# Scan of a two-layer backbone on one core: the order of two products, and level evictions of only the changed columns

## The reference

```python
def wkv_scan(state, r, w, k, v, a, b, reverse):
    def step(s, inp):
        r_t, w_t, k_t, v_t, a_t, b_t = inp
        sa = jnp.einsum('bhij,bhj->bhi', s, a_t)
        s = s * w_t[:, :, None, :] + sa[..., None] * b_t[:, :, None, :] + v_t[..., None] * k_t[:, :, None, :]
        return s, jnp.einsum('bhij,bhj->bhi', s, r_t)
    tm = lambda t: jnp.swapaxes(t, 0, 1).astype(jnp.float32)
    state, y = lax.scan(step, state, tuple(tm(t) for t in (r, w, k, v, a, b)), reverse=reverse)
    return state, jnp.swapaxes(y, 0, 1)
```

## Time and profile before

| | us |
|---|---|
| median of 3 runs | 2361.94 (2360.23 to 2364.19) |
| the profiled execution | 2363.53 |
| its span, first to last instruction | 2361.7 |
| first and last r of the scan begin (line 2023) | 1284.6 and 2213.7 |
| period, m4 to m4, latent | 11.80 |
| mean granted TensorE clock | 0.972 of full |

### The profile page before, as it was taken

How to read it: one execution, slowest core, us unless ns; L and a number is a source line. 1 busy time by engine, 2 the same in 40 slices (tenths; PEclk the granted TensorE clock), 3 DMA queues, 4 the chain that set the end, 5 groups by cost and what they waited for, 6 DMA issues and landing times. The chain is left out here.

```text
span 2361.7 us, 56008 instructions
## 1 busy us (share of the span) xinstructions
PE 2152.6 (91%) x23820; PEld 1377.2 (58%) x23820; DVE 1160.8 (49%) x2245; ACT 803.0 (34%) x2060; POOL 623.4 (26%) x882
## 2 busy tenths in 40 slices
PE   7999999999699989999895898999999898989798
PEld 3556555355344444544344777777777777777543
DVE  4122122134647670042523666666666666666574
ACT  4111111133245522210112444444444544444332
POOL 0000000023022410011113444444444444444111
PEclk9999999999799999999996999999999999999899
DMA  8200002600027755455313343333333333333542
GB/s 350 112 27 27 18 27 80 232 27 27 30 65 209 196 139 180 146 176 187 133 60 112 83 151 88 88 89 94 85 96 85 92 86 89 87 89 79 188 142 107
DMA packets 313562, 258.50 MB, mean 109 GB/s; under 512 B 138593, under 2 KB 271969, under 8 KB 309858
## 3 DMA queue, kind: packets, MB, share of 16 engines
q1 hardware_dynamic: 313314, 254.92, 35.8%
HBM read 175.13 MB, written 79.69 MB: 108 GB/s over the span
## 5 line engine op out<-in xcount | busy, mean ns | idle before, releaser
L876 PE MATMUL ps<-xt,w_slab 128*128 128x512 f32 (+1 forms) x832 | 312.0, 529 | 10.2 <-DVE xt L1156 10.2
L432 PE MATMUL ps<-h,fw_slab 128*128 128x512 f32 (+1 forms) x768 | 282.0, 527 | 2.1 <-ACT h L259 2.1
L1973 PE MATMUL ps<-M,AT 64*64 64x64 f32 x6400 | 272.0, 225 | 5.0 <-DVE M L1860 2.1
L1719 POOL TENSOR_TENSOR SP<-Q,decay 64x128 f32<-64x128 f32 x304 | 139.2, 458 | 467.2 <-DVE Q L1900 438.0
L876 PEld LDWEIGHTS ps<-xt,w_slab 128*128 128x128 f32 x832 | 155.6, 191 | 162.9 <-issue 136.4
L1973 PEld LDWEIGHTS ps<-M,AT 64*64 64x64 f32 x6400 | 221.3, 136 | 48.5 <-issue 14.9
L1973 PE MATMUL ps<-TT,MT 64*64 64x64 f32 x5120 | 218.0, 225 | 20.4 <-ACT XT L1781 15.3
L432 PEld LDWEIGHTS ps<-h,fw_slab 128*128 128x128 f32 x768 | 145.7, 191 | 133.0 <-issue 125.4
L1973 PEld LDWEIGHTS ps<-TT,MT 64*64 64x64 f32 x5120 | 179.2, 136 | 51.3 <-issue 38.2
L1846 DVE COPY_PREDICATED TT<-mask,ps 128x256 f32<-128x256 int32 x400 | 167.2, 435 | 77.3 <-PE ps L1973 74.7
L1889 DVE STREAM_TRANSPOSE MT<-M 128x256 f32<-128x256 f32 x240 | 106.9, 445 | 148.9 <-ACT M L1781 146.4
(11 more groups left out here) (266 smaller groups left out, 3187.0 us busy)
## 6 DMA issues: line engine op xcount, KB each, us to landing
feat<-feature_scratch SPq DMA_DIRECT2D x160, 256.0 KB, 3.2
feature_scratch<-k_feats SPq DMA_DIRECT2D x64, 320.0 KB, 5.1
feature_scratch<-k_feats SPq DMA_DIRECT2D x24, 640.0 KB, 6.7
k_feats<-in_modw SPq DMA_DIRECT2D x8, 1536.0 KB, 6.4
w_slab<-in_rwin SPq DMA_DIRECT2D x24, 512.0 KB, 6.8
Q<-v_token_scratch SPq DMA_DIRECT2D x320, 32.0 KB, 2.5
Z<-v_token_scratch SPq DMA_DIRECT2D x320, 32.0 KB, 2.2
fgo<-in_modw SPq DMA_DIRECT2D x8, 1024.0 KB, 7.8
```

The costliest lines, as they stand in the source:

```text
L432: mm = pe.matmul(ps[:, b0 + b, 0:n], wi[:, half, k, :], h0[:, k, a:a + n], start=k == 0, stop=k == KT - 1)
L876: mm = pe.matmul(ps[:, bank, 0:n], w[:, i % 2, k, :], src[:, k, a:a + n], start=k == 0, stop=k == KT - 1)
L1719: g.tensor_tensor(SP[own(h)], turn(sub, Q[l][own(h), h]), pend_turn(c, own(h), sub).unsqueeze(2).broadcast_to([HD, NDIR, CK]), ALU.mult).t ...
L1973: mm = pe.matmul(out[o, b, :], L[o, b, :], R[o, b, :], start=True, stop=True)
```

## The change

1. On PE, `state(j, c, 0)` goes in front of `y_state(j, c, 0)`. The wait for Z goes with it. The second half of the period (sub 1) keeps its order.
2. M and TT tiles are evicted only in the columns that the level changes: in each 2k columns the first k in the forward direction and the second k in reverse, 128 of 256 columns, in runs of k (k = 2, 4, 8, 16, 32). M and TT tiles get k or CK columns of padding so that one access pattern covers both directions. The eviction of mt32 writes 128 columns (runs of 32) into MT, and XT is gone; `sa` reads MT. The mask table shrinks to 256 + 5 x 128 = 896 columns. The masking of MT1, its transpose and the transposes to MT keep their 256 columns.

```diff
+NMASK = 256 + 128 * len(LEVELS)
...
-    maskf = sb("mask_in", [P, 6, 256])
-    mask = sb("mask", [P, 6, 256], I32)
+    maskf = sb("mask_in", [P, NMASK])
+    mask = sb("mask", [P, NMASK], I32)
...
-    AT, MT1, M, MT, XT = ([sb(f"{n}{s}", [P, B4, CK]) for s in two] for n in ("AT", "MT1_", "M", "MT", "XT"))
-    TT = {k: [sb(f"TT{k}_{s}", [P, B4, CK]) for s in two] for k in LEVELS}
+    AT, MT1, MT = ([sb(f"{n}{s}", [P, B4, CK]) for s in two] for n in ("AT", "MT1_", "MT"))
+    M_cols = [sb(f"M{s}", [P, B4 * CK + CK]) for s in two]
+    TT_cols = {k: [sb(f"TT{k}_{s}", [P, B4 * CK + 2 * k]) for s in two] for k in LEVELS}
+    blocks = lambda t: t[:, 0:B4 * CK].rearrange("p (b t) -> p b t", b=B4)
+    M, TT = [blocks(t) for t in M_cols], {k: [blocks(t) for t in TT_cols[k]] for k in LEVELS}
...
+    def changed(t, k):
+
+        by_dir = t[:, 0:B4 * CK + 2 * k].rearrange("p (d x) -> p d x", d=2)[:, :, 0:2 * CK]
+        return by_dir.rearrange("p d (i y) -> p d i y", y=2 * k)[:, :, :, 0:k]
+
+    def runs(t, k):
+        return t.rearrange("p (d i x) -> p d i x", d=2, x=k)
+
+    def x_cols(t):
+
+        return t.rearrange("p b (h x) -> p (b h) x", h=2)[:, 1:7].rearrange("p (d h) x -> p d h x", d=2)[:, :, 0:3:2]
...
-                act.activation(M[par(cc)][:], lev(4), ACT.Copy).then_inc(aa, 1)
+                act.activation(changed(M_cols[par(cc)], 2), changed(ps[:, 4, :], 2), ACT.Copy).then_inc(aa, 1)
...
-                act.activation((XT if name == "xt" else M)[par(cc)][:], lev(5), ACT.Copy).then_inc(ab, 1)
+                if name == "xt":
+                    act.activation(x_cols(MT[par(cc)]), x_cols(lev(5)), ACT.Copy).then_inc(ab, 1)
+                else:
+                    k = int(name[1:])
+                    act.activation(changed(M_cols[par(cc)], k), changed(ps[:, 5, :], k), ACT.Copy).then_inc(ab, 1)
...
-            def masked(o, i, m):
-                return v.copy_predicated(o, mask[:, m, :], i)
+            def masked(k, cc, bank):
+                lo = 256 + LEVELS.index(k) * 128
+                return v.copy_predicated(changed(TT_cols[k][par(cc)], k), runs(mask[:, lo:lo + 128], k), changed(ps[:, bank, :], k))
...
-                    mm = pe.matmul(seq(7)[o, d, :], XT[par(c)][o, at(sub, d), :], Rs[sub][o, d, :], start=True, stop=True)
+                    mm = pe.matmul(seq(7)[o, d, :], MT[par(c)][o, at(sub, d), :], Rs[sub][o, d, :], start=True, stop=True)
...
-                if not is_lat(c):
+                if sub == 0 or not is_lat(c):
                     pe.wait_ge(asa, count("four", j, c, 2 * sub + 2))
...
-                if lat:
-                    y_state(j, c, 0)
                 if Q_:
                     state(j, c, 0)
                 if lat:
+                    y_state(j, c, 0)
                     y(j, c, 0)
```

More of the change, by code:

```diff
@@ L1857, in first_x @@
                 v.wait_ge(aa, count("act_first", j, cc, AA["at1"]))
-                masked(flat(MT1[s][:]), flat(AT[s][:]), 0).then_inc(da, 1)
+                v.copy_predicated(flat(MT1[s][:]), mask[:, 0:256], flat(AT[s][:])).then_inc(da, 1)
                 v.wait_ge(da, count("dve_first", j, cc, DA["mt1"]))
-                v.transpose(flat(M[s][:]), flat(MT1[s][:])).then_inc(da, 1)
+                v.transpose(flat(M[s]), flat(MT1[s][:])).then_inc(da, 1)
             def first_ak(j, cc):
@@ L1876, in first_t @@
                 v.wait_ge(pa, count("first", j, cc, PA[f"t{k}"]))
-                masked(flat(TT[k][par(cc)][:]), ps[:, 4, 0:256], 1 + LEVELS.index(k)).then_inc(da, 1)
+                masked(k, cc, 4).then_inc(da, 1)
             def first_mt2(j, cc):
                 v.wait_ge(aa, count("act_first", j, cc, AA["m2"]))
-                v.transpose(flat(MT[par(cc)][:]), flat(M[par(cc)][:])).then_inc(da, 1)
+                v.transpose(flat(MT[par(cc)][:]), flat(M[par(cc)])).then_inc(da, 1)
             def second_t(j, cc, k):
                 v.wait_ge(pb, count("second", j, cc, PB[f"t{k}"]))
-                masked(flat(TT[k][par(cc)][:]), ps[:, 5, 0:256], 1 + LEVELS.index(k)).then_inc(db, 1)
+                masked(k, cc, 5).then_inc(db, 1)
             def second_mt(j, cc, k):
                 v.wait_ge(ab, count("act_second", j, cc, AB[f"m{k}"]))
-                v.transpose(flat(MT[par(cc)][:]), flat(M[par(cc)][:])).then_inc(db, 1)
+                v.transpose(flat(MT[par(cc)][:]), flat(M[par(cc)])).then_inc(db, 1)
             def state(j, c, sub):
@@ L2149 @@
         dirs(m, (t // (2 * k) == s // (2 * k)) & (s // k % 2 == 0) & (t // k % 2 == 1)) for k, m in zip(LEVELS, low)]
-    smask = np.stack([np.repeat(m, 2, axis=1).reshape(P, 256) for m in tab_levels], axis=1)
+    first_cols = lambda k, d: [c for c in range(CK) if c // k % 2 == d]
+    level_cols = lambda m, k: np.concatenate([m[:, d, first_cols(k, d)] for d in (0, 0, 1, 1)], axis=1)
+    smask = np.concatenate([np.repeat(tab_levels[0], 2, axis=1).reshape(P, 256)] + [level_cols(m, k) for m, k in zip(tab_levels[1:], LEVELS)], axis=1)
     strict, incl = dirs(s < t, s > t), dirs(s <= t, s >= t)
```

## The result

The changed kernel takes 2319.93 us (median of 4 runs, 2317.29 to 2322.26) against 2361.18 for the kernel before (4 runs, 2360.23 to 2364.19). The ratio is 0.9824, 95% interval 0.9808 to 0.9839: 41.2 us faster, where 45.5 were forecast. The profiled execution took 2322.26, its span is 2320.5.

What follows compares the result with a forecast made beforehand. A closed chain of links per scan period, PE busiest at 91%, was taken as the bound. Latent 38.4, context 6.1, start 2.0, less 1.0, made 45.5 us off the profiled 2363.53; median forecast 2316.4, range 2303 to 2338.

Steps and rivals of the forecast that it cites:

- The closed chain of rows 4: In a latent scan period: m4, products, m8, state, DVE's addition, r, t2, m16, XT, back to m4; 11.80 us.
- Part one: PE's state product ahead of y_state in the first half: 0.22 us earlier in 64 latent periods, bounds 0 and 0.38.
- Rival 1: At state and y_state on PE: no price for the shape change, state gains 0.38, 10 us more, 2306; chance 0.12.
- Rival 2: The swap on PE gives nothing, since Y's eviction pushes R or the addition waits for y; 2331, chance 0.14.
- Part two: Half the columns in ACT evictions and DVE masked copies: chain links TT16, M of m16, TT32, XT; 0.38 us a period.
- one of the prediction's own signs of being wrong: Wrong if DVE's masked copies of k=2 and k=32 differ widely; they were expected near 290 ns for every k.
- Its reading of Door 1: An access crossing into a new 16-byte line pays; with runs of 2, m2 and t2 would gain less than estimated.
- Rivals 3 and 4: Part two gives nothing, 2348, chance 0.08; or ACT and DVE pay for every run, the chain grows, 2405, chance 0.05.
- Rival 5: The chain is tied elsewhere, so the gain comes back as a longer wait, for POOL's operands say; 2362, chance 0.03.
- The step that failed: At the eviction of M16: 0.11 gained in full, the state addition behind the transpose being ready then.
- The late transfer: One 6.1 us wait for a late feature transfer swallows what some 1.5 periods gain before it, 0.6.
- The start of the scan: Ahead of the scan, smaller mask table, int conversion and shorter first-chunk evictions: 2 us, between 1 and 3.

Runs made afterwards that it cites:

- e5: The changed kernel with state in front of y_state in the second half of the period too; 2330.13 us, ratio 0.9861.
- e1: The kernel before with only the state product moved in front of y_state, evictions of 256 columns; 2348.02 us against 2360.79, ratio 0.9946.

## Why the prediction was right, and where its sum was off

**What bounds.** The closed chain of rows 4 was right: every link that was to get shorter did so by what it was priced at, within 0.01. One link was to stay as it was and didn't; it is the step below. PE's work never became the bound.

**Part one, 0.22 a latent period.** Measured 0.23, and 12.8 us for the swap alone where 14.1 stood in the sum. The price of 0.15 per change of tile shape held three times in the new order, and e5 shows it as a loss where no idle time hides it. Rival 1, no such price, needed 0.38. Rival 2, a part one that gives nothing, is out by e1, and its place, Y in front of R on ACT, by the rows: R began 0.49 after r, and 0.50 before. The slack there was as thin as reckoned, 0.13 us.

**Part two, 0.38 a period.** Measured 0.32 in latent periods (0.55 less part one's 0.23), 24.3 us for the columns alone. The price per instruction held for ACT (277 ns for 275) and for DVE at levels 16 and 32; at level 2 the masked copy cost what the full one did. So one of the prediction's own signs of being wrong did show: the copies were not near 290 ns for every k, that of level 2 took 0.44 us where those of levels 32 and 4 took 0.54 together. It didn't hurt the sum, since the prediction had left that copy out of the chain. Its reading of Door 1 in the Trainium skill, "SBUF — State Buffer", was half of what stands there: the page asks for two hits in a 16-byte line, which a run of 2 words gives, so that page doesn't foretell the dear copy. Rivals 3 and 4 are out: at runs of 16 and 32 nothing is dear. Rival 5 is out with the 41.2 us.

**The step that failed** is one sentence, that behind M16 "the state addition ... is ready then". It was ready at the very moment at which the transpose let go, so the addition was no longer queued and took 0.61 instead of 0.57 (in e5, where state comes earlier, it is 0.57 again): 0.04 x 48 periods, 1.9 us, and 2.4 with the 0.01 that the other links of a latent period lack in sum. Period 9 gave 0.51 where 0.60 was reckoned (its copy at 0.50 instead of 0.41 beside POOL), 0.6 over the seven groups that have it; context periods gave 0.37 for 0.38, 0.2. The prediction had no term for POOL. The third group as a whole shows 5.13 for 5.56, and 0.43 x 8 is 3.5 of the 4.3 us missing.

**The rest.** The late transfer swallowed 1.1 instead of 0.6: periods 0 and 1 of group 1 grew from 28.89 to 29.24 while their kind shrank by 0.73. That is another 0.5 of the 4.3. The start of the scan was put at 2; in the profiled pair the first r begins 2.8 earlier, but that point moves by several us from run to run, so the 2 is neither borne out nor refuted.

## What to carry to other kernels

In a scan whose periods repeat, write the period as a closed chain of links; a shorter instruction pays only as a link, and only until the next releaser stands level with it, so two gains at one join don't add. When products of different tile shape are reordered, count the changes of shape, and put the extra ones where PE would wait anyway. A large load that is needed much later goes out in pieces: here, in one piece, it delayed the small ones that were needed at once and cost the clock as well, 7.6 us in all. A gain that falls short in one period of several alike is a reason to look at what the other engines do there.

## What the runs showed of the hardware that was not expected

- A masked copy on DVE that writes runs of 2 columns takes 0.43 us for 128 columns, 0.29 contiguous and 0.33 with both sides in runs of 4; the plain copy writes runs of 2 in 0.32 or less. Half the columns in runs of 2 saved nothing over the full 256 (0.44 against 0.435). In a queue the next instruction starts only 0.04 us later for it.
- A masked copy of 256 columns between SBUF tiles takes 0.85 instead of 0.44 us while POOL works in SBUF, and POOL's operation 0.79 instead of 0.61; with its source in PSUM the copy takes 0.43 and POOL 0.61. In the scan this moved one copy between 0.41 and 0.90 us by the moment at which it met POOL, and made the two parts of the change give 4 us more together than one by one.
- Two DVE additions in a queue take 0.57 us, and 0.61 when the first has to wait for PE.
